# Four mixed expert rounds: the first round of a top-2-of-8 MoE pairs a wide and a narrow expert, seven experts are ranked, and the weight ring has nine tiles

## The reference

```python
D_MODEL = 1024; SEQ = 256; N_EXPERTS = 8; TOP_K = 2; EXPERT_DIM = 3584

def swiglu(h, w_gate, w_up, w_down):
    return (jax.nn.silu(h @ w_gate) * (h @ w_up)) @ w_down

def moe_swiglu(h, w_router, w_gate, w_up, w_down):
    """Top-2-of-8 routed SwiGLU (softmax over the selected logits)."""
    logits = (h @ w_router).astype(jnp.float32)
    top_val, top_idx = lax.top_k(logits, TOP_K)
    top_w = jax.nn.softmax(top_val, axis=-1)
    gates = jnp.sum(jax.nn.one_hot(top_idx, N_EXPERTS, dtype=jnp.float32) * top_w[..., None], axis=-2)
    out = jnp.zeros_like(h)
    for e in range(N_EXPERTS):
        y = swiglu(h, w_gate[e], w_up[e], w_down[e])
        out = out + gates[..., e:e + 1].astype(h.dtype) * y
    return out
```

## Time and profile before

| | us |
|---|---|
| median of 3 runs | 2011.33 |
| profiled execution, its own time | 2010.12 |
| its span | 2008.3 |
| PE busy | 1968.5 (98%) |
| DVE busy | 1297.4 (65%) |
| ACT busy | 1139.1 (57%) |
| granted TensorE clock, mean | 0.997 |
| HBM read | 536.32 MB, 270 GB/s over the span |

### The profile page before, as it was taken

One profiled execution on the slowest core, in us unless ns is written; L12 is line 12 of the kernel. 1 busy time (PEld: TensorE's weight loads), 2 busy tenths in 40 slices (PEclk: granted clock), 3 DMA queues, 4 the chain that ended last, 5 costly groups with the idle time before them and its releaser, 6 DMA issues.

```text
span 2008.3 us, 26407 instructions
## 1 busy us (share of the span) xinstructions
PE 1968.5 (98%) x9966; PEld 1513.4 (75%) x9967; DVE 1297.4 (65%) x1990; ACT 1139.1 (57%) x1830; POOL 70.8 (4%) x93
## 2 busy tenths in 40 slices
PE   9999999999999999999999988999999999999998
PEld 7788888878888766576667655878777888878787
DVE  5665557779999744474447224986666776665776
ACT  6564446667787644474336224774556655556674
POOL 0000000034000000000000000000100000020000
PEclk9999999999999999999999999999999999999999
DMA  7356555259999899999999999955444455544443
GB/s 287 127 192 233 187 187 180 84 224 377 369 384 368 353 412 421 421 414 406 421 421 421 404 421 421 420 212 196 153 164 144 142 181 180 182 148 161 146 149 105
DMA packets 79336, 543.07 MB, mean 270 GB/s; under 512 B 11034, under 2 KB 11290, under 8 KB 14561
## 3 DMA queue, kind: packets, MB, share of 16 engines
q1 hardware_dynamic: 78240, 539.40, 69.4%
q0 software_dynamic: 816, 1.79, 0.2%
q10 hardware_dynamic: 144, 0.10, 0.0%
HBM read 536.32 MB, written 6.03 MB: 270 GB/s over the span
## 4 chain that ended last, share of the span: by engine, by line
PE 85%; DMA 7%; DVE 3%; ACT 2%; issue 1%; SPq 0%; ACTq 0%; DVEq 0%; POOLq 0%
PE bank L249 23%; PE bank L251 22%; PE bank L250 22%; PE bank L2101 6%; PE bank L813 4%; DMA ring_wide<-in_moe_tiles 3%; DMA moe_ring<-in_moe_tiles 3%; PE bank L2111 2%; DVE w_low L224 1%; ACT w_high L216 1%; DVE w_low L227 1%; PE bank L3032 1%; DMA ring<-in_moe_tiles 1%; PE bank L2026 1%; PE bank L3054 0%
## 5 line engine op out<-in xcount | busy, mean ns | idle before, releaser
L249 PE MATMUL bank<-w_high,xT_high 128*128 128x512 f32 x1072 | 426.7, 398 | 1.8 <-DVE xT_low L528 0.9
L251 PE MATMUL bank<-w_high,xT_low 128*128 128x512 f32 x1072 | 418.4, 390 | 1.6 <-issue 1.6
L250 PE MATMUL bank<-w_low,xT_high 128*128 128x512 f32 x1072 | 417.7, 390 | 0.0
L224 DVE TENSOR_TENSOR w_low<-ring,w_high 128x1024 fp32r<-128x1024 f32 x195 | 240.5, 1233 | 205.4 <-ACT w_high L216 203.6
L216 ACT ACTIVATE w_high<-ring 128x1024 fp32r<-128x1024 f32 x195 | 206.3, 1058 | 200.3 <-PE bank L251 182.4
L227 DVE TENSOR_TENSOR w_low<-ring,w_high 128x1024 fp32r<-128x1024 f32 x195 | 239.8, 1230 | 0.1
L249 PEld LDWEIGHTS bank<-w_high,xT_high 128*128 128x128 f32 x1072 | 201.4, 188 | 47.2 <-issue 6.6
L249 PE MATMUL bank<-w_high,moe_x_high 128*128 128x512 f32 x560 | 227.2, 406 | 7.1 <-DVE w_low L224 7.1
L251 PEld LDWEIGHTS bank<-w_high,xT_low 128*128 128x128 f32 x1072 | 201.2, 188 | 43.2
L250 PEld LDWEIGHTS bank<-w_low,xT_high 128*128 128x128 f32 x1072 | 201.6, 188 | 39.0
L251 PE MATMUL bank<-w_high,moe_x_low 128*128 128x512 f32 x560 | 219.7, 392 | 0.0
(11 more groups left out here) (424 smaller groups left out, 3045.3 us busy)
## 6 DMA issues: line engine op xcount, KB each, us to landing
moe_ring<-in_moe_tiles SPq DMA_DIRECT2D x144, 1024.0 KB, 11.8
ring<-in_hy_tiles SPq DMA_DIRECT2D x103, 1024.0 KB, 4.8
ring<-in_moe_tiles SPq DMA_DIRECT2D x96, 1024.0 KB, 10.3
ring_wide<-in_moe_tiles SPq DMA_DIRECT2D x96, 1024.0 KB, 11.0
ring<-in_ffn_tiles SPq DMA_DIRECT2D x17, 1024.0 KB, 4.7
ring_wide<-in_ffn_tiles SPq DMA_DIRECT2D x16, 1024.0 KB, 4.8
ring_wide<-in_gla_in_tiles SPq DMA_DIRECT2D x6, 1024.0 KB, 9.7
ring<-in_sb_in_tiles SPq DMA_DIRECT2D x6, 1024.0 KB, 4.8
```

Of the source, the lines that this page charges most:

```text
L224: self.nc.vector.tensor_tensor(self.low[:, place, FIRST], memory[:, FIRST], self.high[:, place, FIRST].bitcast(F32), ALU.subtract).then_in ...
L249: nc.tensor.matmul(out, x[0], w[0], start=start, stop=False, **more)
L250: nc.tensor.matmul(out, x[0], w[1], start=False, stop=False, **more)
L251: return nc.tensor.matmul(out, x[1], w[0], start=False, stop=stop, **more)
```

## The change

It does five things. (1) Round 0 pairs a wide and a narrow expert: `NARROW` becomes (0, 2, 4, 6), expert 0 is always at place 1 (wide), experts 1 to 7 are ranked and the four smallest go to the narrow places. (2) Round 0 begins with `LEAD` = 5 wide steps of expert 0, whose tiles (0 to 13) SP can issue without the table; the 14 narrow steps are spread over the steps 5 to 23. (3) The narrow expert's tokens of round 0 are gathered late: POOL orders `slot_of` by place first, DVE builds the selection in step 2 (`make_few_sel`), PE gathers in step 4 (`few_gather`), ACT copies (`few_gathered_act`). (4) The ring has nine tiles (`MOE_RING`), and the last 12 tiles go round in six of them, so that the first three buffers come free for the next layer. For this the gathered tokens `xg` share memory with `K.xT`, and `by_place` and `place_of` are laid out anew. (5) POOL's ranking works on 8x8 instead of 6x6.

```diff
-RANKED = N_EXPERTS - 2
-RANK_AT = (1, 3, 0, 4, 2, 5)
-NARROW = (2, 4, 6)
-FEW_BY = {2: 24, 4: 24, 6: 18}
+RANK_AT = (4, 0, 2, 5, 1, 6, 3, 7)
+NARROW = (0, 2, 4, 6)
+FEW_BY = {0: 24, 2: 24, 4: 24, 6: 18}
+LEAD = 5
-MOE_RING = 7
+MOE_RING = 9
...
     def __init__(self, few_by=None, lead=0):
...
-            done = [i * N // few_by for i in range(few_by + 1)]
-            kinds = [done[i + 1] - done[i] for i in range(few_by)] + [0] * (2 * N - few_by)
+            span = few_by - lead
+            done = [i * N // span for i in range(span + 1)]
+            kinds = [0] * lead + [done[i + 1] - done[i] for i in range(span)] + [0] * (2 * N - few_by)
...
+        self.put_at = (8, 4) if lead else (6, 6)
...
+    LAST = PAIRS * PER - 2 * (MOE_RING - SPLIT)
+    def slot_at(v):
+        if v < LAST:
+            return v % MOE_RING
+        return SPLIT + (v - LAST) % (MOE_RING - SPLIT) if v < PAIRS * PER else v - PAIRS * PER
...
+        rounds = [Round(FEW_BY.get(2 * n), 0 if n else LEAD) for n in range(PAIRS)]
+        STATIC = number["guA", LEAD]
+        for u in order[RING_WIDE:STATIC]:
+            W.plan(slots, tile_parts(expert_tile(K, 0, *u)))
...
                 sync.wait_ge(W.used, K.t_sb_out[0] + 3)
+                W.issue(sync, W.cursor["dve"], first + MOE_RING - 2)
+                sync.wait_ge(W.used, K.t_sb_out[0] + 4)
                 W.issue(sync, W.cursor["dve"])
...
-        xg = (sb("x_high", [P, KC, 2 * P], F32R), sb("x_low", [P, KC, 2 * P], F32R))
+        xg = K.xT
...
+        def make_few_sel(dve):
+            dve.wait_ge(experts_placed.sem, experts_placed.at(1))
+            for t in range(TT):
+                ins = nc.vector.tensor_scalar(sel[:, t, P:].rearrange("p (h n) -> p h n", h=2), slot_numbers[:, 0:FEW].unsqueeze(1).broadcast_to([P, 2, FEW]),
+                                              placed["slot_of"][:, t, 0:1], None, ALU.is_equal)
+            ins.then_inc(first_sel.sem, 1)
+
+        def few_gather(pe):
+            pe.wait_ge(first_sel.sem, first_sel.at(2))
+            for k in range(KC):
+                for t in range(TT):
+                    for i in range(2):
+                        last = nc.tensor.matmul(B[2][:, k * FEW:(k + 1) * FEW], rows[i][:, t, k * P:(k + 1) * P], sel[:, t, P:P + FEW],
+                                                start=((i, t) == (0, 0)), stop=((i, t) == (1, 1)))
+            last.then_inc(few_gathered.sem, 1)
+
+        def few_gathered_act(act):
+            act.wait_ge(few_gathered.sem, few_gathered.at(1))
+            nc.scalar.activation(x_few.rearrange("p k n -> p (k n)"), B[2][:], ACT.Copy).then_inc(few_ready.sem, 1)
...
             def row_and_gate(q):
+                if pair == 0:
+                    pe.wait_ge(experts_placed.sem, experts_placed.at(2))
...
+            pool.wait_ge(first_sel.sem, first_sel.at(1))
+            by_places(placed["slot_of"], posm[:, :, 0:E])
+            pool.sem_inc(experts_placed.sem, 1)
             pool.wait_ge(rows_numbered.sem, rows_numbered.at(1))
...
-                W.issue(sync, first + PER)
+                W.issue(sync, first + STATIC)
                 overflows["SP"] = overflowing(K, sync, table)
-                placed_expert = [0, 1] + [sync.value_load(...) for m in range(2, E)]
+                placed_expert = [0 if m == 1 else sync.value_load(...) for m in range(E)]
...
-                for pair in range(1, PAIRS):
-                    for u in range(PER):
+                for pair in range(PAIRS):
+                    for u in range(0 if pair else STATIC, PER):
...
-                            rows_in={3: lambda: rows_and_gates(dve)} if pair == 0 else {} if more else add_at(dve))
+                            rows_in={LEAD - 3: lambda: make_few_sel(dve), LEAD - 2: lambda: rows_and_gates(dve)} if pair == 0 else {} if more else add_at(dve))
```

More of the change, by code:

```diff
@@ L1850, with __init__ @@
 class ExpertSems:
-    def __init__(self, nc, ctx, prefix, stream, first, value, scattered_before, put=0, splits=None, free=None, hh_at=None, unsplit=None):
+    def __init__(self, nc, ctx, prefix, stream, first, value, scattered_before, put=0, splits=None, free=None, hh_at=None, unsplit=None, memory=None):
         (self.sel, self.gath, self.xh, self.xg, self.silu, self.hid, self.tp, self.hh, self.hT, self.ya, self.yv, self.gps,
@@ L1862, in __init__ @@
         self.put = put
-        self.splits, self.free, self.hh_at, self.unsplit = splits, free, hh_at, unsplit
+        self.splits, self.free, self.hh_at, self.unsplit, self.memory = splits, free, hh_at, unsplit, memory
     def multiplied(self, m):
@@ L1958, in moe @@
         plain = Round()
-        rounds = [Round(FEW_BY.get(2 * n)) for n in range(PAIRS)]
         over_tile = lambda n, u: (n + u // PER, u % PER)
@@ L2190, in pe_run @@
                 q, c = r.seq[s]
[L2191 removed]
+                if put[q] and c == r.put_at[q]:
                     row_and_gate(q)
@@ L2195, in pe_run, with act_run @@
             down(STEPS - 1)
-        def act_run(act, G, n, last_tile, late, put=(False, False), r=plain):
+        def act_run(act, G, n, last_tile, late, put=(False, False), beside={}, r=plain):
             def used(kind, s):
@@ L2242, in act_run @@
                     turned(s - 1)
-                if put[q] and c == PUT_AT + 1:
+                if s in beside:
+                    beside[s](act)
+                if put[q] and c == r.put_at[q] + 1:
                     act.wait_ge(G.gst, r.place(n, q) + 1)
@@ L2409, in load @@
                 def load(pair, u, src):
-                    n, v = divmod(pair * PER + u - MOE_RING, PER)
+                    n, v = divmod(previous[pair * PER + u], PER)
+                    memory, name, _ = runs[pair * PER + u]
                     if narrow_tile(n, v):
@@ L2779, in _ @@
                 halves = over.rearrange("p (n q) -> p n q", q=2)
-                before, behind = order_of[:, 0], order_of[:, 1]
-                low, square = E - RANKED, [P, RANKED, RANKED]
-                counts = ct[:, 0, low:E]
-                key = over[:, 0:RANKED]
+                before, behind, square = tie[:, 0], tie[:, 1], [P, E, E]
+                counts, key, place = ct[:, 0, :], over, at
+                along, down = (lambda x: x.unsqueeze(1).broadcast_to(square)), (lambda x: x.unsqueeze(2).broadcast_to(square))
@@ L2788, in _ @@
                 then(nc.gpsimd.tensor_scalar(before, before, 0.0, None, ALU.is_gt))
[L2789 to L2791 removed]
+                total(nc, then, place, before)
+                then(nc.gpsimd.tensor_tensor(behind, along(place), down(K.const("rank_at")), ALU.subtract))
```

149 lines of the change are left out of this document (75 added, 74 removed).

## The result

The changed kernel takes 1980.64 us (median of 4 runs, 1980.57 to 1981.38) against 2011.3 us (2010.44 to 2012.79) on the same chip: a ratio of 0.9847, 95% interval 0.9832 to 0.9862. Predicted were 1984 us. The profiled execution took 1980.57 us, its span 1978.8, 29.5 us less than before.

The account below looks back on a forecast made before the run. PE was taken to bound round 0, the transfers rounds 1 and 2. Terms -26.1 - 2 + 0 + 1 = -27.1 us took the profiled 2010.12 us to 1983.0; with the median 1.2 us higher, 1984 us, range 1975 to 1996.

Parts of the forecast that it names:

- (a): Round 0 becomes mixed and takes 213.2 us instead of 239.25: 26.1 us less, ends 30 and 20 less.
- the same mix under the same limit: Round 0: rounds 1 and 2 taken as the nearest thing measured, so it takes their mean, 213.2 us.
- (b): Ring of nine: 2 us less over the changes of round, at most 8, at least none; nothing before round 0.
- 1 us per change of round: Rounds 1 and 2: two more buffers gain 1 us at each change of round, 2 us in all.
- 8.0 us lost to standstill: Rounds 1 and 2: 8.0 us lost while transfers stood still, the most the ring of nine could gain.
- (c): SP's wait for POOL's table between tiles 13 and 14: tile 14 out at about 458.5 us, no cost.
- one us per us from 460 on: Tile 14 behind the table: free if SP is free by about 460 us, then about one us lost per us.
- The rival of a late table: POOL slows among DVE's splits, tile 14 goes out at about 470 us, some 10 us lost: 1994 us; chance 0.10.
- (d): DVE waits for slot_of before its product of step 2, and PE for DVE: 1 us more, ends 0 and 3.
- (e): Round 0's row_and_gate waits for POOL's last order, in step 11 or later; smaller store of rows: nothing for either.
- my last test: Whole kernel: the prediction is wrong if the gain lies outside the mixture.
- The transfers as a bound already in the old round 0: Rival: round 0 already transfer-bound, nothing gained by mixing; 2011 us or slower by (c) and (d); chance 0.02.

Follow-up runs that it names:

- the run with 473.3 us: Also called the late table: changed kernel with 32 more small POOL operations ahead of the table, tile 14 out at 473.31 us; 1990.76 us.
- the three edits: Changed kernel with round 0's narrow steps sooner, round 3's over 20 steps with later read-backs, and row_of_norm behind the next layer's first tile; 1989.53 us.
- the changed kernel again: The changed kernel run and traced once more, unchanged, beside three other runs on one chip (its second trace); 1981.45 us.

## Why the prediction was right or wrong

**(a) Round 0 becomes mixed: -26.1 predicted, as what rounds 1 and 2 took.** The time of the round came out (213.68 for 213.2), but the edit alone does not make it. With the old ring the mixed round 0 takes 221.33 us, 17.9 less than the wide one, or 19.5 without the 1.6 us of its longer gather: beyond the end of 20 that I had set. The step that failed is "the same mix under the same limit": round 0 has PE, with five wide steps, a sixth from the even spread, and the gather ahead of its first narrow tile, as its limit until tile 17 is released. (The first narrow step is step 6, and tile 17 its first tile; the part on the change says step 5.) Two readings under this term were off without bearing on it: the slices of round 0 alone read 368 to 384 GB/s, not 369, and the 181.2 us of waiting leave out the 20.4 us for round 1's tiles.

**(b) The ring: -2 predicted, ends 0 and -8.** The words "they serve the same purpose there, and I count nothing for them" failed. The two more tiles on hand ahead of round 0 are worth 6.1 us in it; with the rest of the mixture and the longer gather of that run the ring is worth 9.9 us (some 8 if that gather's 1.6 us of half clock, which no run shows to be the ring's doing, are left out), and in the kernel with a wide round 0 up to 7.6. Of the "1 us per change of round" 1.3 and 1.9 were measured. Part of the "8.0 us lost to standstill" was never standstill: round 1 moves 89.22 MB, of which tiles are 88.08, and 89.22 MB at 421 GB/s are 211.9 us, what it now takes. Stores of rows and loads of instructions make up the other 1.14 MB, so the floor was 212 and not 209.2. The two errors, 8 us too much in (a) and 8 too little in (b), cancel, and that the total came out is luck to that extent. The span shrank by 29.5 us against 27.1 predicted; the 1 us of (d) and the 1.6 us outside the mixture make up that difference, to 0.2 us. The upper end of the terms was also added wrongly: 2011.3 - 20 + 10 + 3 is 2004, not 2001; the range given ended below both.

**(c) The table: 0 predicted.** Tile 14 went out at 456.53 us instead of the 458.5 reckoned: the table stood at 451.4, two us sooner. The bound "one us per us from 460 on" is wrong: a tile 14 at 464.4 us costs nothing to speak of, and in the run with 473.3 us it is the late selection that costs. The rival of a late table needed POOL to be late by that much, and its price would have come through DVE.

**(d) The late gather's wait: 1 predicted, 0 measured;** its 3.8 us of PE were 3.5. I had set them beside a nearly even bound of the transfers; runs with an eighth and three times of it show that each us of it is paid.

**(e) Nothing predicted.** Nothing seen.

Of the signs named in advance, the distance of 213.68 us, the landing time, tile 14 by 460, the product of step 2 by 463 (461.80) and the last ten steps at 8.4 us (75.59 us for nine) came; so did SP's shorter wait, 168.1 us for 201.6, and the rate at the changes of round, 419 to 421 GB/s. The rate of round 0 stayed at 402 GB/s, under the 405 that were wanted. At 421 GB/s that is 9.6 us of transfers lost: 5.7 in the two standstills, 2.2 between 456 and 462 us behind the stop at the table, the rest ahead of it.

**Outside the mixture** 1.6 us were gained, against my last test, and the traces show where. Some 22 us behind the last silu, in the first matmuls of the next layer, PE stands in the kernel before with no wait that the profile shows:

```profile
1341.06 0.39 PE L251 MATMUL bank<-w_high,xT_low 128*128 128x512 f32 x1 [1.62 <-issue]
```

The run with a wide round 0 has such a stop of 1.53 us (rest 690.7), the one with the gather thrice the 3.71 us shown above; the other eleven traces, the changed kernel's two among them, have none, and their rest is 689.1 to 690.0 us but for the disturbed end of the three edits. So the 1.6 us are this stop. It goes neither with the order of the last buffers nor with a narrow round 0 alone; why PE stands there stays open, and the prediction had no term for it.

The transfers as a bound already in the old round 0 are refuted: once the experts are mixed the same 84 tiles pass in 213.68 us at 402 GB/s, while a ring of nine with wide experts, where PE is busy for 239.05 us, takes the same 239.25 us. The prediction set the 358 GB/s per core of the Trainium skill, DMA: Bandwidth & Descriptors, section Where 436 GB/s comes from, against the trace; the Trainium skill, HBM Reference, section Specifications (TRN2), says further that a core streaming alone reaches about 425. The 421 GB/s over rounds 1 and 2 agree with that sentence.

## What to carry to other kernels

Where two stages with different bounds follow each other, the stock of buffers at their border was worth about its own transfer time, once (6.1 and 5.4 us here for two tiles of 2.49), and an edit that moves a stage from one bound to the other changes what every buffer is worth: price them together, and test each alone even when the total comes out. A DMA floor is all bytes of the stretch over the highest rate seen, not the large tiles alone. Ask of a buffer not only how many there are but what releases it: one that is held until its use ties the next transfer to the slowest step ahead of that use.

## What was not expected of the hardware

**Half clock under full work.** In seven of the twelve traces that have a late gather, PE's clock fell to its lower level during or just behind it, and the step took 13.5 to 13.6 us instead of 11.97 (25.56 with the gather thrice); by the profile PE had been busy without a gap. The run with the ring of seven beside the changed kernel again, the same 4 us:

```profile
478.00:482.00 4.00, 4.00 (x14) 3.21 (x13) 2.28 (x3) 2.76 (x4) 1.68 (x8) 0.64 1.01 426
```

```profile
478.00:482.00 4.00, 4.00 (x20) 3.34 (x20) 2.18 (x3) 3.61 (x6) 1.98 (x9) 1.00 0.99 414
```

The Trainium skill, TensorE: Matmul & The Clock Gate, section Part 1: The HAM clock gate, has activity release the clock and idleness lower it. The trace disagrees here: the clock fell under or right behind back-to-back matmuls of 64 columns, each with its weight load. No run varied the columns or the weight loads, so the cause is not shown. It does not fall in every execution: the two traces of the changed kernel have it at 1.00 there. And it costs only where PE is the bound. In the changed kernel's second trace the clock is 0.72 between 600 and 606 us, and step 21 takes 10.30 us instead of 8.74; but step 22 then takes 6.82 instead of 8.38, and PE's wait for the split of a late tile there (1.68 us at 615.04 us in the first trace) is gone: the slower matmuls used time that was idle.

**POOL beside DVE.** The four operations that order `slot_of` take 1.49, 1.19, 1.30 and 1.08 us beside DVE's splits. With DVE waiting, in the run with the late table, the first and last of the same four:

```profile
468.24 0.43 POOL L2413 TENSOR_TENSOR moe_sel_weighted<-moe_ahead,moe_slot_of 128x128 f32<-128x128 f32 x1
...
469.46 0.21 POOL L2569 TENSOR_TENSOR moe_by_place<-moe_sel_weighted 128x16 f32<-128x16 f32 x1
```

The Trainium skill, SBUF — State Buffer, section SBUF: two separate sides, has an operation of DVE with two inputs from SBUF and one of POOL exclude each other. The trace agrees: each operation of POOL takes 0.9 to 1.1 us more beside the splits, nearly one split of 1.2 us.
